# One Trainium2 core, float32r matmuls in three passes: the order of the passes inside a feature slab

## What is computed

```
h = h + 0.5 * swiglu(rmsnorm(h), w_gate, w_up, w_down)          # ffn1, inner width 2816
h = h + mixer_1(rmsnorm(h) @ w_in) @ w_out                      # window attention + gated linear attention
h = h + 0.5 * swiglu(rmsnorm(h), ...)                           # ffn2
h = h + sigmoid(rmsnorm(h) @ w_ple) * rmsnorm(p @ w_proj)
for l in 0, 1:
    h = h + mixer_2(rmsnorm(h))                                 # differential / stick-breaking attention
    h = h + cross_attention(rmsnorm(h), rmsnorm(mem))
    h = h + (silu(conv(up)) * conv(up')) @ w_down               # conv_ffn, inner width 2816
```

## Time and profile before

| | us |
|---|---|
| median of 3 runs | 2555.47 (2555.09 to 2555.61) |
| profiled execution, its own time | 2556.16 |
| span of the profiled execution | 2554.3 |
| TensorE matmul busy in it | 2535.7 (99%), 12612 matmuls |
| VectorE busy | 1600.2 (63%) |
| ScalarE busy | 921.1 (36%) |
| granted TensorE clock, mean | 0.999 |

### The profile page before, as it was taken

The page is one execution under the profiler, slowest core; times in us unless marked ns, Lnnn a source line. Parts: engine busy times, 40 slices in busy tenths (PEclk is TensorE's granted clock), DMA queues, the critical chain, the costliest instruction groups (busy, mean ns, idle before and its releaser), DMA issues.

```text
span 2554.3 us, 32136 instructions
## 1 busy us (share of the span) xinstructions
PE 2535.7 (99%) x12612; PEld 2105.5 (82%) x12612; DVE 1600.2 (63%) x1992; ACT 921.1 (36%) x1200; POOL 10.2 (0%) x24
## 2 busy tenths in 40 slices
PE   8999999999999999999999999999999999999999
PEld 7888888778888888877898888888887889888887
DVE  6444468866444468677775747476357666775755
ACT  5222234543222145344453323233146344432322
POOL 0000001000000000000000000000000000000000
PEclk9999999999999999999999999999999999999999
DMA  5222233112222232312332222323210232232322
GB/s 185 99 84 99 96 110 121 67 50 93 104 93 99 99 115 101 99 50 99 122 109 71 96 99 84 113 83 123 95 67 2 98 116 83 84 116 82 102 96 83
DMA packets 37411, 241.93 MB, mean 95 GB/s; under 512 B 4416, under 2 KB 7280, under 8 KB 9136
## 3 DMA queue, kind: packets, MB, share of 16 engines
q1 hardware_dynamic: 34736, 233.78, 26.8%
q10 hardware_dynamic: 1920, 5.22, 0.6%
q0 software_dynamic: 640, 1.31, 0.2%
HBM read 236.89 MB, written 2.10 MB: 94 GB/s over the span
## 4 chain that ended last, share of the span: by engine, by line
PE 93%; DVE 4%; ACT 1%; issue 1%; DMA 0%; DVEq 0%; ACTq 0%
PE ps L621 24%; PE ps L622 24%; PE ps L623 24%; PE ps L639 1%; PE ps L641 1%; PE ps L640 1%; PE ps L1211 1%; PE ps L1290 1%; PE ps L1314 1%; PE ps L1305 1%; PE ps L782 1%; PE ps L784 1%; PE ps L783 1%; PE ps L1326 1%; PE ps L832 1%
## 5 line engine op out<-in xcount | busy, mean ns | idle before, releaser
L621 PE MATMUL ps<-op_hi,w_hi 128*128 128x512 f32 x2056 | 800.7, 389 | 0.2 <-DVE op_lo L1965 0.2
L622 PE MATMUL ps<-op_lo,w_hi 128*128 128x512 f32 x2056 | 800.2, 389 | 0.0
L623 PE MATMUL ps<-op_hi,w_lo 128*128 128x512 f32 x2056 | 799.9, 389 | 0.0
L1373 ACT ACTIVATE w_hi<-w_raw 128x2048 fp32r<-128x2048 f32 x217 | 414.3, 1910 | 475.7 <-PE ps L623 292.0
L2084 DVE TENSOR_TENSOR w_lo<-w_raw,w_hi 128x2048 fp32r<-128x2048 f32 x217 | 497.0, 2292 | 33.9 <-ACT w_hi L1373 16.8
L621 PEld LDWEIGHTS ps<-op_hi,w_hi 128*128 128x128 f32 x2056 | 386.0, 188 | 81.5 <-issue 1.4
L623 PEld LDWEIGHTS ps<-op_hi,w_lo 128*128 128x128 f32 x2056 | 386.0, 188 | 80.7
L622 PEld LDWEIGHTS ps<-op_lo,w_hi 128*128 128x128 f32 x2056 | 386.0, 188 | 79.9
L2049 DVE SCALAR_TENSOR_TENSOR x<-ps,x 128x512 f32<-128x512 f32 x134 | 92.6, 691 | 312.9 <-PE ps L623 294.8
L621 PE MATMUL ps<-h_hi,w_hi 128*128 128x512 f32 x692 | 269.5, 389 | 0.0
L623 PE MATMUL ps<-h_hi,w_lo 128*128 128x512 f32 x692 | 269.2, 389 | 0.0
(11 more groups left out here) (382 smaller groups left out, 3116.8 us busy)
## 6 DMA issues: line engine op xcount, KB each, us to landing
w_raw<-in_wstream_dram SPq DMA_DIRECT2D x217, 1024.0 KB, 4.9
cr_m<-in_mem_dram ACTq DMA_DIRECT2D x2, 1024.0 KB, 5.0
w_raw<-in_wstream_dram SPq DMA_DIRECT2D x7, 256.0 KB, 7.5
x<-in_x_dram SPq DMA_DIRECT2D x3, 512.0 KB, 6.9
out_dram<-x SPq DMA_DIRECT2D x3, 512.0 KB, 2.6
m_s<-m_q POOLq DMA_DIRECT2D x16, 64.0 KB, 2.8
ev_s<-in_alibi_dram ACTq DMA_DIRECT2D x1, 1024.0 KB, 4.9
m_c<-in_rope_dram ACTq DMA_DIRECT2D x1, 640.0 KB, 4.1
```

The costliest lines, as they stand in the source:

```text
L621: mm_(o, w_hi[:, c % 4, w], hi[:, k, 0:cols], start=(k == 0), stop=False)
L622: mm_(o, w_hi[:, c % 4, w], lo[:, k, 0:cols], start=False, stop=False)
L623: mm = mm_(o, w_lo[:, c % 4, w], hi[:, k, 0:cols], start=False, stop=(k == kt - 1))
L1373: f_(w_hi[:, c % 4, :], w_raw[:, c % 2, :], ACT.Copy).then_inc(w_hi_ready, 1)
```

## The change

Feature slabs that are neither `pieces` nor `last` go to a new function. In it the passes of w_hi (four matmuls per tile) come first, over all tiles; then the passes of w_lo, all tiles of output 0 and then all tiles of output 1. The wait for `w_ready` moves from the slab's start to the first w_lo pass, and the start waits for `w_hi_ready` instead. Loads, VectorE, ScalarE and GpSimd do what they did.

```diff
@@ -606,6 +606,9 @@
                             pieces=False, js=(0, 1), between=None, between_at=1):
 
 
+                if not pieces and not last:
+                    high_products_first(c, off, hi, lo, kt, cols, wait, js, between, between_at)
+                    return
                 if not pieces:
                     start_slab(c, off)
                 for k in range(kt):
@@ -625,6 +628,27 @@
                         mm.then_inc(op_used, 1)
                     if between is not None and k == between_at:
                         between()
+                mm.then_inc(slab_done, 1)
+
+            def high_products_first(c, off, hi, lo, kt, cols, wait, js, between, between_at):
+
+                pe.wait_ge(w_hi_ready, off + (c + 1))
+                same = pair_of(c) == pair_of(c - 1)
+                pe.wait_ge(acc_free, off + (c + (2 if same else 1)))
+                for k in range(kt):
+                    if wait is not None:
+                        pe.wait_ge(wait[0], wait[1] + (k + 1))
+                    for j in js:
+                        o, w = acc(c, j)[:, 0:cols], slice((j * kt + k) * P, (j * kt + k + 1) * P)
+                        mm_(o, w_hi[:, c % 4, w], hi[:, k, 0:cols], start=(k == 0), stop=False)
+                        mm_(o, w_hi[:, c % 4, w], lo[:, k, 0:cols], start=False, stop=False)
+                    if between is not None and k == between_at:
+                        between()
+                pe.wait_ge(w_ready, off + (c + 1))
+                for j in js:
+                    for k in range(kt):
+                        o, w = acc(c, j)[:, 0:cols], slice((j * kt + k) * P, (j * kt + k + 1) * P)
+                        mm = mm_(o, w_lo[:, c % 4, w], hi[:, k, 0:cols], start=False, stop=(k == kt - 1))
                 mm.then_inc(slab_done, 1)
 
             def to_positions(c, cols=256, beside={}):
```

## The result

| | before | changed |
|---|---|---|
| median, us | 2555.54 (2555.09 to 2556.06, 4 runs) | 2580.53 (2578.84 to 2581.01, 4 runs) |
| ratio, 95% interval | | 1.0096 [1.0084, 1.0108] |
| profiled execution, its own time, us | 2556.16 | 2578.84 |
| its span, us | 2554.3 | 2577.0 |
| granted TensorE clock, mean | 0.999 | 0.999 |

The changed kernel is 25 us, 1.0%, slower. Predicted were 2581.6 us and a range of 2574 to 2588.

The account below looks back on a forecast made before the run. TensorE was taken as the bound throughout. To the profiled 2556.16 us came 21.0 of idle time with waking up and 5.1 for the clock, 2582.3, or 2581.6 us by the median; range 2574 to 2588.

Parts of the forecast that it names:

- The bound and the mechanism: TensorE, busy 99%, bounds the kernel throughout; tiles asked for after 4 matmuls each instead of 6 leave unrecovered idle time.
- The last tile of a 6-tile slab: Conv MLP down slabs: tile lands at 6.77 us, asked for at 4.53 instead of 6.80; 2.24 us late, twice.
- waking up: After each of 13 stalls TensorE restarts late, 0.2 us each; 2.3 us in all after what two slabs already pay.
- The stalls: New TensorE idle time in 13 places, conv MLP down slabs and first slabs of stages: 18.7 us.
- rival (5): More stalls, from a further wait in a chain such as the squares' sum, or a longer slow stretch: 2588 to 2595; 3%.
- The even mixer: First slab: eighth tile lands at 8.36 us but is asked for at 6.35, 2.01 us of idle time.
- the moved `w_ready` wait: Wait for w_lo, 32 matmuls later in an 8-tile slab, saves 0 and costs 0, as TensorE never waited for it.
- the new sequence of passes: Feature slabs: the distance between matmuls stays at 226.7 ns when a low pass follows a low pass; no change.
- (2): Matmul distance worsens to the embeddings' 233.4 ns over 7908 passes, 53 us more, about 2634 us; 6%.
- (3): Low passes run closer, 13.3 ns saved on each of 2636, 35 us, giving 2547 us, faster; 4%.
- (4): No new idle time, because activations land earlier than in the trace; within 5 us of before; 2%.
- The clock: Lower TensorE clock (1.2 GHz) after three of five idle spells of about 2 us, 1.7 us each: 5.1 us.

Follow-up runs that it names:

- experiment 1: The changed kernel, but the 22 slabs that wait tile by tile keep the old order: 2555.6 us, ratio 0.9999.
- experiment 2: The mirror: against the kernel before, new order only in the 22 slabs that wait tile by tile: 2581.07 us, ratio 1.0099.
- experiment 4: The changed kernel, but in slabs waiting tile by tile the low passes of all other tiles go ahead of the last tile: 2566.1 us, ratio 1.0043.
- experiment 3: The changed kernel with the wait for `w_ready` back at the start of the slab: 2581.14 us, ratio 1.0101.
- experiment 8: The changed kernel with extra matmuls, whose result nobody reads, in the five new stalls of 2 us, second measurement: 2577.95 us.
- experiment 9: The changed kernel measured again, unaltered, beside the one with extra matmuls in the five long stalls: 2580.34 us.

## Why the prediction was right

**The bound and the mechanism** held: TensorE stays the bound, the order costs through the time at which tiles are asked for, and experiments 1, 2 and 4 show it from three sides. The last tile of a 6-tile slab asked for at 4.53 us instead of 6.80 costs what the subtraction said, within 0.06 us, and this 0.06 is the first part of waking up.

**The stalls.** Predicted 18.7 us in 13 places, measured 19.3 in the same 13 with the first part of waking up. Waking up in all was put at 2.3; it is 0.8 + 1.6 = 2.4. One place was left out: the first slab of the odd mixer's output projection, which also waits for `op_ready`. Its last tile ended at 2003.31 + 0.69 = 2004.00 (next rows) while the 29th matmul was due at 2003.77; 0.29 us. The `sum_rows` asked for earlier, rival (5), cost 0.15 in one place.

```profile
2003.31 0.69 DVE L1965 TENSOR_TENSOR op_lo<-ps,op_hi 128x512 fp32r<-128x512 f32 x1
...
2003.54 0.40 PE L644 MATMUL ps<-op_lo,w_hi 128*128 128x512 f32 x1
2004.06 0.50 PE L643 MATMUL ps<-op_hi,w_hi 128*128 128x512 f32 x1
```

**The even mixer** has its 2.01 as 0.15 + 1.66: a wait for the fourth tile comes first, and what is idled there is no longer missing at the eighth. The sum holds, within 0.2.

**What was costed at nothing** was nothing: the moved `w_ready` wait (experiment 3) and the new sequence of passes (226.7 ns; experiment 1). Rivals (2), (3) and (4) fell. The rule of the Trainium skill ("TensorE: Matmul & The Clock Gate", section "Wait — 56ns, not 53.3ns?", 215.7 ns for 512 columns back to back) doesn't describe this kernel's passes in either order; the trace says 226.7.

**The clock was the mis-sized term.** I took three of five stalls at 1.7 us, 5.1 us, on top of the one that the kernel before has. Over five traces it is two of five, and a stretch costs 1.6 us in the slabs and 1.1 behind `od_lo` (experiments 8 and 9). So the price was nearly right for the slabs, and the count too high. (Behind `od_lo`, where the price was read off the mean clock of a window, 1.7 was too much: the traces with and without the stretch differ by 1.1.) In the profiled execution it was one new stretch, while the old one behind `od_lo` happened not to come. So against the profiled execution the sum (2582.3) was 3.5 us too high: the clock term too high by some 4.6 (5.1 against 1.6 less 1.1), the start longer by 0.6, the rest the place left out. Against the median (2581.6 against 2580.5) it was 1.1 too high. That is less because most runs of the changed kernel are at mean clock 0.998, and the traces at 0.998 have two new stretches, 3.2 us, beside the one behind `od_lo`. How many come in an execution the prediction could not know; that the median lies so near is in part luck.

## To carry to other kernels

When TensorE is the bound and a slab's operands arrive one after another, ask of each reordering how much work stands ahead of the last arrival: work put behind it can't hide the wait. Putting passes with an early operand first pays only where the other operand is really waited for, and the view of waits says so before anything is built (here it had no line for `w_lo`). Where a helper serves waiting and non-waiting slabs alike, sort the call sites by what they wait for: nearly nine tenths of this change were free, and 22 slabs made all of its cost.

## What was not expected of the hardware

- The same stall of 2.2 to 2.35 us is followed by a stretch at the lower clock level in one execution and not in the next, and by place very unevenly: PLE in 5 of the 5 traces with all the stalls (but not in that of experiment 4), mixer 1, nearly as long, in none. The places go together in an execution. The runs of the changed kernel fall into clusters by it: 2575.65 to 2576.90 us at a mean clock of 1.000, 2580.1 to 2581.0 at 0.998, and three between, 2578.8, at 0.999.
- A transient follows a stall: the first matmul's successor comes 0.33 us later, and the next eight or so 224 to 236 ns apart, before the distance is back at 226.7 ns.
- One to six matmuls of the first slab run at the lower clock level in the traces with the old start, 0.2 us more each, which alone moves two executions of one kernel by up to 1 us.
